# One quarter in four of an S5 table generated on GpSimd instead of VectorE, and the S5 sample state loaded chunk by chunk

## The reference

```
h    = rmsnorm(x) * (1 + sc1) + sh1             # sc, sh, gt: adaLN vectors from c
u, v, s, gA, gB = split(h @ w_in)               # 1024 -> 5 x 1024
y_a  = gelu(u) * (tril(W_s) norm(gelu(v)) + b)  # in chunks of 128 positions
bu   = einsum(s, b_bar)                         # 64 groups of 16 channels, 64 complex states each
bu[:, 0] += a_bar * h0                          # sample group only: h0 is the incoming state
hs   = scan(h_t = a_bar * h_{t-1} + bu_t)
y_b  = glu(gelu(Re(C hs) + d * s))              # last state is an output too
x   += gt1 * ((sigmoid(gA) * y_a + sigmoid(gB) * y_b) @ w_out)
x   += gt2 * (relu(rmsnorm'(x) @ w_ff1)**2 @ w_ff2)
```

## Time and profile before

| | |
|---|---|
| median of the runs shown | 3773.32 us (3769.74 and 3776.90) |
| the profiled execution | 3770.98 us |
| its span, first to last instruction, slowest core (1) | 3769.4 us |
| spans of the 8 cores | 3758.9 to 3769.4 us |
| granted TensorE clock, mean of each core | 0.823 to 0.825 |
| TensorE busy | 2505.5 us (66%) |
| VectorE busy | 1811.7 us (48%) |
| ScalarE busy | 1197.4 us (32%) |
| GpSimd busy | 787.5 us (21%) |

### The profile page before, as it was taken

One profiled execution on the slowest core, in us unless ns is written; L12 is line 12 of the kernel. 1 busy time (PEld: TensorE's weight loads), 2 busy tenths in 40 slices (PEclk: granted clock), 3 DMA queues, 4 the chain that ended last, 5 costly groups with the idle time before them and its releaser, 6 DMA issues.

```text
span 3769.4 us, 52299 instructions; the slowest of 8 cores (3758.9 to 3769.4 us)
## 1 busy us (share of the span) xinstructions
PE 2505.5 (66%) x17688; PEld 1259.3 (33%) x17688; DVE 1811.7 (48%) x3309; ACT 1197.4 (32%) x1741; POOL 787.5 (21%) x1200
## 2 busy tenths in 40 slices
PE   0268986610559959999526898660056986999950
PEld 0023445510224424444212344550023432444420
DVE  1342257787772352334424226778677244333431
ACT  0279912200343232210027981220034324221022
POOL 2200012258331101111220011226832110111100
PEclk9999986655779969999758998665577997999975
DMA  9902231000013314333990132100001331334311
GB/s 172 96 3 18 27 35 14 7 6 1 5 14 34 34 12 39 38 37 43 83 94 3 18 35 27 14 7 6 1 5 14 34 34 15 37 37 39 37 36 60
DMA packets 383061, 120.05 MB, mean 32 GB/s; under 512 B 370352, under 2 KB 371760, under 8 KB 382800
## 3 DMA queue, kind: packets, MB, share of 16 engines
q0 software_dynamic: 351648, 92.30, 25.8%
q1 hardware_dynamic: 31152, 24.40, 2.2%
HBM read 199.24 MB, written 9.70 MB: 55 GB/s over the span
## 4 chain that ended last, share of the span: by engine, by line
PE 54%; DVE 13%; POOL 9%; issue 8%; DMA 8%; ACT 6%; DVEq 0%; POOLq 0%; ACTq 0%; SPq 0%
PE ps L390 42%; DMA sb_wts<-w_ada 6%; PE ps L598 3%; PE ps L656 3%; DMA yT<-sb_tbf 2%; DVE sb_bB L502 2%; DVE sb_tmp L503 2%; DVE sb_tmp L501 2%; DVE sb_tmp L504 2%; DVE sb_tmp L500 2%; PE ps L330 2%; POOL sb_gcur L487 2%; DVE sb_tmp L342 1%; POOL sb_nrm L726 1%; ACT sb_sq L328 1%
## 5 line engine op out<-in xcount | busy, mean ns | idle before, releaser
L390 PE MATMUL ps<-sb_hb,sb_wts 128*128 128x512 bf16 (+1 forms) x4480 | 847.6, 343 | 16.1 <-ACT sb_tmp L837 6.4
L390 PEld LDWEIGHTS ps<-sb_hb,sb_wts 128*128 128x128 bf16 x4480 | 376.4, 98 | 447.1 <-issue 46.7
L400 DVE SCALAR_TENSOR_TENSOR sb_x<-ps,sb_mod,sb_x 128x512 f32<-128x512 f32 x384 | 288.2, 751 | 352.0 <-PE ps L390 352.0
L390 PE MATMUL ps<-sb_bB,sb_wts 128*128 128x512 bf16 (+1 forms) x2560 | 456.1, 337 | 0.0
L773 PE MATMUL ps<-sb_bA,sb_bB 128*128 128x512 bf16 (+3 forms) x640 | 155.6, 399 | 342.0 <-DVE sb_bB L754 342.0
L390 PE MATMUL ps<-sb_bA,sb_wts 128*128 128x512 bf16 (+1 forms) x1920 | 356.4, 338 | 13.8 <-ACT sb_bA L796 13.8
L932 ACT ACTIVATE sb_tbf<-ps 128x512 bf16<-128x512 f32 (+1 forms) x320 | 157.4, 513 | 529.1 <-PE ps L390 521.5
L316 POOL DMA_DIRECT2D sb_wts<-w_ff x128 | 111.9, 874 | 940.6 <-PE ps L390 927.9
L390 PEld LDWEIGHTS ps<-sb_bB,sb_wts 128*128 128x128 bf16 x2560 | 213.7, 97 | 241.9
L330 PE MATMUL ps<-sb_sq,sb_ones_m 128*128 128x512 bf16 (+1 forms) x200 | 91.2, 482 | 268.9 <-ACT sb_sq L328 256.3
L390 PEld LDWEIGHTS ps<-sb_bA,sb_wts 128*128 128x128 bf16 x1920 | 161.6, 97 | 197.3 <-issue 17.0
(11 more groups left out here) (182 smaller groups left out, 3625.2 us busy)
## 6 DMA issues: line engine op xcount, KB each, us to landing
sb_wts<-w_ff POOLq DMA_DIRECT2D x128, 256.0 KB, 4.5
sb_wts<-w_ada POOLq DMA_DIRECT2D x96, 256.0 KB, 7.8
sb_wts<-w_in POOLq DMA_DIRECT2D x64, 256.0 KB, 5.3
sb_x<-xT SPq DMA_DIRECT2D x32, 256.0 KB, 12.4
sb_wts<-w_out POOLq DMA_DIRECT2D x32, 256.0 KB, 4.7
yT<-sb_tbf SPq DMA_DIRECT2D x32, 256.0 KB, 2.1
sb_bB<-w_in POOLq DMA_DIRECT2D x2, 2048.0 KB, 21.2
sb_wts<-w_glu POOLq DMA_DIRECT2D x16, 256.0 KB, 4.6
```

The source lines that it names most:

```text
L390: P.op("pe", lambda h, s=s, k=k, K=K, src=src, t0=t0, tn=tn, bank=bank: h.matmul(pst[bank][:, 0:tn], lhsT=wts[:, s, k, :], rhs=bufk(src, k ...
L400: P.op("dve", lambda h: h.scalar_tensor_tensor(out=xk(m, t0, tn), in0=pst[bank][:, 0:tn], scalar=mod[:, 0, g, 0:1], in1=xk(m, t0, tn), op0 ...
```

## The change

Three edits, all in the S5 branch. (1) Instead of the whole `h0`, each chunk's 128 columns are loaded: in `sample_state(k)` by SyncE in float32 (`h0k32`), and at the head of each chunk of stage B by GpSimd with conversion to bfloat16 (`h0kb`). The load and the copy at the start of the branch are gone. (2) In stage A quarter 2, and in stage B quarter 3, is generated on GpSimd. (3) On GpSimd `gen_quarter` has its scratch in `tbf`, which edit 1 has freed.

```diff
     def gen_quarter(eng, k, qq, X_re, X_im, Y_re, Y_im, out_re, out_im, reads, writes):
...
+        if eng == "dve":
+            ta_, tb_, r1, r2 = T_A, T_B, ["tmp32_0"], ["tmp32_1"]
+        else:
+            ta_, tb_, r1, r2 = tbf[:, 0:512], tbf[:, 512:1024], ["tb0", "tb1"], ["tb2", "tb3"]
...
     def s5_layer(l):
-        P.op("sp", lambda h: h.dma_start(out=h0f.rearrange("p g r t -> p (g r t)"), in_=h0_d[l]), writes=["tb0", "tb1", "tb2", "tb3"], dma_key="h0")
-        dv(lambda h: h.tensor_copy(out=h0b, in_=h0f), ["tb0", "tb1", "tb2", "tb3"], ["sq0", "sq1"])
...
-            gen_quarter("dve", k, qq, X0, X1, X0, X1, arGW[:, :, 0, :], arGW[:, :, 1, :], ["gX"], [gwr, "arKTx"])
+            gen_quarter("pool" if qq == 2 else "dve", k, qq, X0, X1, X0, X1, arGW[:, :, 0, :], arGW[:, :, 1, :], ["gX"], [gwr, "arKTx"])
...
         def sample_state(k):
-            h0k = h0f[:, 4 * k:4 * k + 4, :, :]
+            P.op("sp", lambda h: h.dma_start(out=h0k32[:].rearrange("p q r t -> p (q r t)"), in_=h0_d[l, :, 128 * k:128 * k + 128]), writes=["h0k32"], dma_key="h0k32")
+            h0k = h0k32[:]
...
         for k in range(8):
+            P.op("pool", lambda h, k=k: h.dma_start(out=h0kb[:].rearrange("p q r t -> p (q r t)"), in_=h0_d[l, :, 128 * k:128 * k + 128]), writes=["h0kb"], dma_key="h0kb")
...
             for qq in range(4):
-                gen_quarter("dve", k, qq, X0, X1, X2, X3, arT[:, 4 * qq:4 * qq + 4, 0, :], arT[:, 4 * qq:4 * qq + 4, 1, :], ["gX"], ["arT%d" % qq])
+                gen_quarter("pool" if qq == 3 else "dve", k, qq, X0, X1, X2, X3, arT[:, 4 * qq:4 * qq + 4, 0, :], arT[:, 4 * qq:4 * qq + 4, 1, :], ["gX"], ["arT%d" % qq])
...
-                        pst[ys][32 * q:32 * q + 32, 0:16], lhsT=arT[:, 0, ri, 32 * q:32 * q + 32], rhs=h0b[:, 4 * k + q, ri, :],
+                        pst[ys][32 * q:32 * q + 32, 0:16], lhsT=arT[:, 0, ri, 32 * q:32 * q + 32], rhs=h0kb[:, q, ri, :],
...
-                        reads=["arT0", "sq0", "sq1"], writes=["ps%d" % ys])
+                        reads=["arT0", "h0kb"], writes=["ps%d" % ys])
```

More of the change, by code:

```diff
@@ L230, in build_nc @@
     smt = sb("smt", [128, 320], F32)
+    h0k32 = sb("h0k32", [128, 4, 2, 16], F32)
+    h0kb = sb("h0kb", [128, 4, 2, 16], BF16)
     BCk = sb("BCk", [128, 2, 2, 64], F32)
@@ L494, in gen_quarter @@
         ai_ = apw[:, 1, 4 * qq:4 * qq + 4, 4 * k:4 * k + 4].unsqueeze(3).to_broadcast([128, 4, 4, 32])
-        t1 = T_A.rearrange("p (t q m) -> p t q m", t=4, q=4)
-        t2 = T_B.rearrange("p (t q m) -> p t q m", t=4, q=4)
+        if eng == "dve":
+            ta_, tb_, r1, r2 = T_A, T_B, ["tmp32_0"], ["tmp32_1"]
+        else:
+            ta_, tb_, r1, r2 = tbf[:, 0:512], tbf[:, 512:1024], ["tb0", "tb1"], ["tb2", "tb3"]
+        t1 = ta_.rearrange("p (t q m) -> p t q m", t=4, q=4)
+        t2 = tb_.rearrange("p (t q m) -> p t q m", t=4, q=4)
         bx = lambda X: X.rearrange("p (q m) -> p q m", q=4).unsqueeze(1).to_broadcast([128, 4, 4, 32])
@@ L499, in gen_quarter @@
         rd = reads + ["apw"]
[L500 to L505, removed]
+        dv(lambda h: h.tensor_tensor(out=t1, in0=ar_, in1=bx(X_re), op=ALU.mult), rd, r1, eng)
+        dv(lambda h: h.tensor_tensor(out=t2, in0=ai_, in1=bx(X_im), op=ALU.mult), rd, r2, eng)
+        dv(lambda h: h.tensor_tensor(out=o4(out_re), in0=t1, in1=t2, op=ALU.subtract), r1 + r2, writes, eng)
+        dv(lambda h: h.tensor_tensor(out=t1, in0=ar_, in1=bx(Y_im), op=ALU.mult), rd, r1, eng)
+        dv(lambda h: h.tensor_tensor(out=t2, in0=ai_, in1=bx(Y_re), op=ALU.mult), rd, r2, eng)
+        dv(lambda h: h.tensor_tensor(out=o4(out_im), in0=t1, in1=t2, op=ALU.add), r1 + r2, writes, eng)
     def s5_tables(l):
@@ L681, in sample_state @@
             HN = ["msb", "rstd"]
-            dv(lambda h: h.tensor_tensor(out=t13, in0=h0k, in1=arb, op=ALU.mult), ["tb0", "tb1", "tb2", "tb3", "apw"], ["smt"], "pool")
-            dv(lambda h: h.tensor_tensor(out=t24, in0=h0k, in1=aib, op=ALU.mult), ["tb0", "tb1", "tb2", "tb3", "apw"], ["smt"], "pool")
+            dv(lambda h: h.tensor_tensor(out=t13, in0=h0k, in1=arb, op=ALU.mult), ["h0k32", "apw"], ["smt"], "pool")
+            dv(lambda h: h.tensor_tensor(out=t24, in0=h0k, in1=aib, op=ALU.mult), ["h0k32", "apw"], ["smt"], "pool")
             dv(lambda h: h.tensor_tensor(out=Sk, in0=Sk, in1=t13, op=ALU.add), ["smt"] + HN, HN, "pool")
```

## The result

| | before | after |
|---|---|---|
| median of all runs, us | 3779.95 (10 runs) | 3904.02 (11 runs) |
| ratio, 95% interval | 1 | 1.0327 (1.0305 to 1.035) |
| the profiled execution, us | 3770.98 | 3908.88 |
| its span on the slowest core, us | 3769.4 (core 1) | 3907.3 (core 5) |
| mean granted TensorE clock, by core | 0.823 to 0.825 | 0.812 to 0.814 |

The kernel is 3.3% slower; 3902 us were predicted. Applied to the profiled 3771 us it gives 3894, which is 123 us more (115 to 132 over its interval); the profiled execution after was itself 138 us longer than the one before. The changed file has more lines, so the numbers shift: L500 to L505 are now L506 to L511, L754 is L760, L773 is L779, L780 is L786, L784 is L790, L788 is L794, L479 is L481, L487 is L489, L598 is L602, L636 is L640, L642 is L646, L645 is L649.

A forecast was written before the change was run, and what follows sets the result against it. VectorE was taken to pace stage B. Seven boundaries of 4.6 + 4.0 + 0.3, 0.7 first chunk and 4.6 last make 67.6 a layer; two layers less 4 give +131 on 3771: 3902 us, wide range 3830 to 3945.

The forecast's parts named there:

- The bound: Stage B: VectorE sets the pace, busy 146 of 179 us against TensorE's 103.
- Stage A, nothing but the first chunk: Stage A: GpSimd's quarter 2 hides under sproj; only the first chunk gains, about 2 us, 4 us in all.
- The load's wait: Stage B chunk start: GpSimd's h0kb load waits for TensorE to end the previous chunk, delaying quarter 0 by 4.6 us.
- The tail: Stage B chunk end: block 3's large matmuls lose quarter 3's cover; 5.0 us instead of 1.01, +4.0 us.
- Contention: Stage B quarter 0: VectorE and GpSimd operations alternate, 1.53 us a pair; three quarters take 18.0 against 17.7 for four.
- The sum: Whole kernel: 67.6 us a layer, two layers 135, less 4 in stage A: +131 on 3771, 3902 us.
- new issue: Stage B, first chunk: only the issue of GpSimd's h0kb load is added, behind the chain, +0.7 us.
- Free contention: Rival, stage B: contention is nearly free, three quarters take 13.2 us, 77 us less, 3825 us; chance 0.09.
- no binding wait: Rival, stage B: the load goes out early, factors ready as L754 ends, 64 us less, 3838 us; chance 0.06.
- the pace of VectorE: Rival, stage B chunk boundary: VectorE keeps setting the pace, each chunk loses one quarter, 70 us, 3697 us; chance 0.04.
- Dearer contention: Rival, stage B: operations hold the port throughout, a pair 1.79 us, 3926 or 3940 us; chance 0.17 including a slower tail.
- the slower clock: Rival, stage B tail: large matmuls at the lower clock take 0.42 us each, 48 us more, 3950; within the 0.17.

The follow-up runs named there:

- run with the mask on ScalarE: Against the run with stage A ahead: ScalarE instead of VectorE's L754 makes stage B's masked table for the next chunk; ratio to before 0.9728, 3672.69 us median.
- run with both mended: Changed kernel with two alternating tiles for h0kb and stage B's quarter 3 back on VectorE; ratio to before 1.0005.
- run with two tiles: Changed kernel with h0kb alternating between the two halves of sq, quarter 3 still on GpSimd; ratio to before 1.0136.
- run with stage A ahead: Against the run with both mended: stage A has quarter 1 instead of 2 on GpSimd, a third tile and a new order; ratio to before 0.9803.

## Why the prediction was right

The mechanism was as told, part by part. How near the total came is in part luck, as the sum below shows.

**The bound.** Stage B was paced by VectorE. The run with the mask on ScalarE bears that out: it takes 2.5 us a chunk off VectorE, and a chunk falls from 21.65 to 20.0 us.

**Stage A, nothing but the first chunk.** Predicted were 2 us a layer, all in the first chunk; the means of eight cores give 1.0 in layer 0 and 0.3 in layer 1. In the first chunk of layer 0, on the slowest cores, evac 3 did begin 2.1 us earlier after `sproj`'s start (8.27 instead of 10.33), but the cast that ends it took 1.18 us beside GpSimd's quarter instead of 0.20, so that 1.0 was left. In the other chunks the differences go from -0.8 to +0.7 us and show nothing.

**The load's wait, +4.6 us.** Measured 7.08 - 2.84 = 4.2. L760 is 0.19 shorter, as no `expand` runs beside it, and GpSimd needed 4.6 us from the end of L481 to quarter 0. The run with quarter 3 back shows it by itself: ratio 1.015, where 1.015 was expected from the measured parts.

**The tail, +4.0 us.** Measured 4.82 - 1.01 = 3.8. It goes away with quarter 3's offload only, as that run shows.

**Contention, +0.3 us.** Measured 18.04 against 17.66: 0.4. A pair took 1.56 us (9.37 / 6) where 1.53 was worked out from the chain. GpSimd's 128x512 operation took 1.05 us, 1.26 to 1.27 with a bfloat16 result; 1.1 had been taken, inside 0.92 to 1.24 on average. The Trainium skill (SBUF — State Buffer, section "SBUF: two separate sides") says that the shared port is held for the whole instruction. By that rule an estimate for a pair with the 1.05 us operation is 1.74 us. The trace agrees with the blocking, but at 1.56 us a pair not with the length of the hold.

**The sum.** A boundary of layer 0 costs 29.90 - 21.65 = 8.25 us on average (six chunks in 179.4 us after, six in 129.9 before), not 8.9. The last chunk, from L760 to ScalarE's last large gelu, takes 29.2 us instead of 20.1 (L754's start at 1103.28 to 1123.38 before, 1159.29 to 1188.53 after): 4.2 for the load and 4.9 where 4.6 was taken. Measured stretch by stretch, as means of eight cores in the two profiled executions:

| us a layer | predicted | layer 0 | layer 1 |
|---|---|---|---|
| first to last `sproj` of stage A | -2.0 | -1.0 | -0.3 |
| last `sproj` to stage B's first quarter (chain, new issue) | +0.7 | +3.5 | +2.1 |
| first quarter to ScalarE's last large gelu | +66.9 | +62.7 | +65.4 |
| together | +65.6 | +65.2 | +67.2 |

Two errors cancel here. Stage B was taken as too dear, by 4 us in layer 0. The stretch with the chain was taken as unchanged but for 0.7 us, and it became 3.5 us longer, of which the new DMA issue is 0.6. No edit touches the chain, and nothing on record says why it takes longer; the run with both mended has the same 3.5 us. That 3902 lies 2 us beside the median of 3904 is luck as well: the runs before the change have a median of 3780, not the 3771 that was added to. The ratio gives 123 us (115 to 132), these stretches 132.

**The rivals.** Free contention, no binding wait and the pace of VectorE all fall to rows of the trace after (1.5 us an operation; GpSimd released by L794; first part 7.08, tail 4.82). Dearer contention falls to the same row: 1.56 us a pair and not 1.79. The tail's large matmuls kept 0.21 us each (16 in 3.31), so the slower clock did not come there; where it did come, behind quarter 0, a large matmul took 0.37 us and not the 0.42 of the rival. The runs also show an interaction that the prediction did not tell: the costs do not simply add. Taking the wait away brings 1.91% and taking the quarter back 1.77%, together 3.68%, while both at once bring 3.22%. The difference, 0.46%, is just outside what the four intervals allow together (0.4%). It fits the trace of the run with two tiles: without the wait GpSimd does part of its quarter under the tail, and that saves 1.4 us a chunk, which the quarter's return makes of no use.

## What to carry to other kernels

Moving work to a second engine costs what it disturbs there and what it uncovers here: a quarter of VectorE's work was also the cover of 16 matmuls, and a small single-buffered load ahead of the factors, in an in-order queue, was enough to put 4 us on every chunk. Ask of each moved piece what was running under it, and of each new load who reads the tile's old contents and what stands behind it in its queue. In this kernel an offload of two-input SBUF operations from VectorE to GpSimd gave back what it took (18.04 us for three quarters beside GpSimd's, 17.66 for four alone). It came with a gain only in stage A, under another engine's wait, together with a buffer more and a reordered list; those three made the kernel 2% faster (1.7 to 2.2), and how much of it the offload brought was not measured by itself.

## What the runs showed of the hardware that was not expected

A cast of VectorE with a single SBUF input is held by GpSimd too: L649, 0.20 us by itself, took 1.18 us in the first chunk of stage A beside a 128x512 operation of GpSimd, and 0.73 us once in the run with stage A ahead. The reduce next to it (PSUM input) kept its 0.69 us. Which of the two starts first matters: in the run with two tiles L760 took 3.37 us instead of 2.29 where a GpSimd operation had started 0.05 us earlier, and at the boundary at 1051.38, where L760 started first, it kept its 2.29 us and GpSimd's operation took 3.12 instead of 1.27. The first chunk of stage A after the change:

```profile
532.32 0.70 DVE L640 TENSOR_TENSOR ps<-ps,sb_bdm 128x512 f32<-128x512 f32 x1 [2.28 <-PE ps L635]
532.60 1.05 POOL L510 TENSOR_TENSOR sb_tbf<-sb_apw,sb_gcur 128x512 f32<-128x512 f32 x1
533.12 0.69 DVE L646 TENSOR_REDUCE sb_smt<-ps 128x64 f32<-128x512 f32 x1
533.79 1.26 POOL L511 TENSOR_TENSOR sb_bB<-sb_tbf 128x512 bf16<-128x512 f32 x1
533.92 1.18 DVE L649 CAST sb_bB<-sb_smt 128x64 bf16<-128x64 f32 x1
```
